# Attention passes: the projection's blocks one block later, and the forget gate's chain spread over four blocks

## What is computed

```python
def mixer_fox_nsa(h, w_in, b_f, cmp_pe, cmp_w1, cmp_w2, w_out):
    proj = h @ w_in
    fq, fk, fv, ff, nq, kc, vc, ks, vs, kw, vw, ng = [proj[..., offs[i]:offs[i + 1]] for i in range(len(IN_SIZES))]
    log_f = jax.nn.log_sigmoid((ff + b_f).astype(jnp.float32))
    o_fox = fox_attention(fq.reshape(hd), fk.reshape(hd), fv.reshape(hd), log_f)
    gates = jax.nn.sigmoid(ng.astype(jnp.float32)).astype(h.dtype).reshape(B, S, NSA_KV_GROUPS, NSA_GROUP_SIZE, 3)
    o_nsa = nsa_attention(nq, kc, vc, ks, vs, kw, vw, gates, cmp_pe, cmp_w1, cmp_w2)
    return jnp.concatenate([o_fox, o_nsa], axis=-1) @ w_out
```

## Time and profile before

| | |
|---|---|
| median of 3 runs | 1832.21 us (1831.14 to 1836.81) |
| the profiled execution | 1836.81 us, span 1835.1 us |
| busy PE / DVE / ACT / POOL | 1723.6 / 911.9 / 657.8 / 183.2 us |
| mean granted PE clock | 0.963 |
| att5 to the last pass, in the trace | about 660 to 975 us |

### The profile page before, as it was taken

One profiled execution on the slowest core, in us unless ns is written; L12 is line 12 of the kernel. 1 busy time (PEld: TensorE's weight loads), 2 busy tenths in 40 slices (PEclk: granted clock), 3 DMA queues, 4 the chain that ended last, 5 costly groups with the idle time before them and its releaser, 6 DMA issues.

```text
span 1835.1 us, 22072 instructions
## 1 busy us (share of the span) xinstructions
PE 1723.6 (94%) x8153; PEld 1348.1 (73%) x8153; DVE 911.9 (50%) x1368; ACT 657.8 (36%) x937; POOL 183.2 (10%) x178
## 2 busy tenths in 40 slices
PE   1999899999999989999999899999999899999996
PEld 1657678888888766666656688888887688888885
DVE  6865674533333361555666644444335744444223
ACT  1324334444322241354555344443224433333221
POOL 4001119910000050000000000001100000000000
PEclk9999889999999989999999799999998799999998
DMA  7554155522322241111102122223222032323221
GB/s 280 206 192 161 47 183 172 179 96 94 118 79 94 73 106 46 58 36 35 36 24 69 58 92 99 95 92 117 95 74 80 12 103 91 103 91 115 93 78 46
DMA packets 49111, 179.73 MB, mean 98 GB/s; under 512 B 5984, under 2 KB 6656, under 8 KB 48928
## 3 DMA queue, kind: packets, MB, share of 16 engines
q1 hardware_dynamic: 44896, 166.75, 27.0%
q0 software_dynamic: 3008, 10.59, 2.1%
q10 hardware_dynamic: 1152, 1.66, 0.3%
HBM read 173.56 MB, written 2.10 MB: 96 GB/s over the span
## 4 chain that ended last, share of the span: by engine, by line
PE 66%; issue 22%; DVE 8%; ACT 2%; DMA 1%; ACTq 1%; POOL 1%; DVEq 0%; POOLq 0%; SPq 0%
PE bank L332 15%; PE bank L333 15%; PE bank L334 15%; PE bank L1195 3%; PE bank L1197 2%; PE bank L1196 2%; PE bank L1299 2%; PE bank L1275 2%; PE bank L1255 1%; DVE ada_acc L1652 1%; PE bank L1180 1%; PE bank L1353 1%; DMA raw<-in_ada_w 1%; DVE w_lo L271 1%; ACT w_hi L267 1%
## 5 line engine op out<-in xcount | busy, mean ns | idle before, releaser
L271 DVE TENSOR_TENSOR w_lo<-raw,w_hi 128x1024 fp32r<-128x1024 f32 (+1 forms) x236 | 319.0, 1352 | 673.2 <-ACT w_hi L267 673.0
L332 PE MATMUL bank<-h_hi,w_hi 128*128 128x512 f32 x1232 | 488.7, 397 | 4.8 <-DVE h_lo L519 1.5
L333 PE MATMUL bank<-h_lo,w_hi 128*128 128x512 f32 x1232 | 482.6, 392 | 0.0
L334 PE MATMUL bank<-h_hi,w_lo 128*128 128x512 f32 x1232 | 481.9, 391 | 0.0
L267 ACT ACTIVATE w_hi<-raw 128x1024 fp32r<-128x1024 f32 (+1 forms) x236 | 265.3, 1124 | 574.0 <-PE bank L334 505.6
L332 PEld LDWEIGHTS bank<-h_hi,w_hi 128*128 128x128 f32 x1232 | 232.8, 189 | 63.1 <-issue 6.4
L334 PEld LDWEIGHTS bank<-h_hi,w_lo 128*128 128x128 f32 x1232 | 233.0, 189 | 49.4
L333 PEld LDWEIGHTS bank<-h_lo,w_hi 128*128 128x128 f32 x1232 | 233.2, 189 | 47.9 <-issue 1.0
L332 PE MATMUL bank<-hid_hi,w_hi 128*128 128x512 f32 x528 | 209.7, 397 | 0.0
L333 PE MATMUL bank<-hid_lo,w_hi 128*128 128x512 f32 x528 | 209.4, 397 | 0.0
L334 PE MATMUL bank<-hid_hi,w_lo 128*128 128x512 f32 x528 | 209.3, 396 | 0.0
(11 more groups left out here) (325 smaller groups left out, 1953.0 us busy)
## 6 DMA issues: line engine op xcount, KB each, us to landing
raw<-in_f2i SPq DMA_DIRECT2D x88, 512.0 KB, 3.2
raw<-in_ffi SPq DMA_DIRECT2D x44, 512.0 KB, 3.3
raw<-in_f2o SPq DMA_DIRECT2D x32, 704.0 KB, 4.0
ada_w<-in_ada_w SPq DMA_DIRECT2D x32, 512.0 KB, 4.0
raw<-in_att_w SPq DMA_DIRECT2D x24, 512.0 KB, 3.2
raw<-in_ffo SPq DMA_DIRECT2D x16, 704.0 KB, 4.0
raw<-in_ada_w SPq DMA_DIRECT2D x16, 512.0 KB, 5.0
raw<-in_w_in SPq DMA_DIRECT2D x16, 512.0 KB, 5.3
```

What stands on the lines that cost most here:

```text
L271: nc.vector.tensor_tensor(WL[par][:, 0:kc * P], RAW[s][:, 0:kc * P], WH[par][:, 0:kc * P].bitcast(F32), ALU.subtract).then_inc(wlo, 1)
L332: pe_.matmul(bank[:, :], w_h, hi[:, k0 + k, :], start=start and k == 0, stop=False)
L333: pe_.matmul(bank[:, :], w_h, lo[:, k0 + k, :], start=False, stop=False)
L334: last = pe_.matmul(bank[:, :], w_l, hi[:, k0 + k, :], start=False, stop=stop and k == kc - 1)
```

## The change

Three things. The passes get a table of steps per slot (STEPS): pass 0 has 24 steps, passes 1 to 3 have 32 of which the first 8 belong to the NQ block of their own pair, and pass 4 has that block's 8. `att_block` stands where the table says a block has ended (`ready_at`), one slot later, except for NQ and for a block that ends in slot 15. In `att_block`, DVE copies the bank out before it makes w_lo. The transposes of V come in slot 1, and DVE's saved output behind the first scores. In att5 PE transposes gates and V one block later, and the forget gate's chain is cut into pieces at blocks (0, 0) to (1, 1).

```diff
+        STEPS = [[2] * 12 + [0] * 4] + [[3, 3, 2, 2, 2, 2, 1, 2, 2, 2, 1, 2, 2, 2, 2, 2]] * 3 + [[3, 3, 2] + [0] * 13]
+        EARLY_AT = 3
+        chunk_of, ready_at, _n = {}, {}, 0
+        for _p in range(5):
+            for _sl in range(SLOTS):
+                chunk_of[_p, _sl] = range(_n, _n + STEPS[_p][_sl])
+                _n += STEPS[_p][_sl]
+                for _s in chunk_of[_p, _sl]:
+                    if _s % C == C - 1:
+                        late = 0 if _s // C % 4 == 3 or _p == 0 or _sl == SLOTS - 1 else 1
+                        ready_at.setdefault((_p, _sl + late), []).append(_s // C)
...
             lin("att5", 0, 2)
+            lin("att5", 0, 3)
             pe_.wait_ge(a5["ng"], 1)
             for i in range(TC):
                 m = pe_.transpose(PS[5][:, i * P:i * P + 3 * NH], NG[:, i * P:(i + 1) * P], IDN[0:3 * NH, 0:3 * NH])
             m.then_inc(a5["ngt"], 1)
-            lin("att5", 0, 3)
...
-            v_turn(VST, PS[4], ev[1], O0["att5"] // 2 + 3, a5["vt"], VF)
...
                 hidden(CMPB - 4, CMPB).then_inc(a5["hc"], 1)
+                if kv == 0:
+                    v_turn(VST, PS[4], ev[1], O0["att5"] // 2 + 3, a5["vt"], VF)
...
-                    if p < 4:
-                        lin_step("att6", 4 * p + sl // 4, 2 * (sl % 4))
-                    elif sl == 1:
+                    steps = chunk_of[p, sl]
+                    ahead = (len(steps) + 1) // 2
+                    for s_ in steps[:ahead]:
+                        lin_step("att6", s_ // C, s_ % C)
+                    if p == 4 and sl == EARLY_AT:
                         pe_.wait_ge(a6["ol"], 6)
-                    if p == 4 and 1 <= sl <= 12:
-                        j, e = divmod(sl - 1, 6)
+                    if p == 4 and EARLY_AT <= sl < EARLY_AT + 12:
+                        j, e = divmod(sl - EARLY_AT, 6)
...
-                        if sl == 0:
+                        if sl == 1:
                             fv_turn(it)
                         if sl < NP_:
                             qk(it, sl)
-                    if p < 4:
-                        lin_step("att6", 4 * p + sl // 4, 2 * (sl % 4) + 1)
+                    for s_ in steps[ahead:]:
+                        lin_step("att6", s_ // C, s_ % C)
...
-                    if sl % 4 == 0:
-                        if sl and p < 4:
-                            att_block(4 * p + sl // 4 - 1)
-                        elif sl == 0 and p:
-                            att_block(4 * p - 1)
+                    for j in ready_at.get((p, sl), ()):
+                        att_block(j)
...
-                split_lo(N0["att6"] + j + 2, t % 2, (t + 2) % 4, C)
                 dve.wait_ge(mm, N0["att6"] + j + 1)
...
+                split_lo(N0["att6"] + j + 2, t % 2, (t + 2) % 4, C)
...
+                        if sl < NP_:
+                            score(it, sl)
                         if sl == 0 and it:
                             out_lo(it - 1, 1)
-                        if sl < NP_:
-                            score(it, sl)
```

More of the change, by code:

```diff
@@ L1483, in beside5 @@
             def beside5(g, t):
-                if (g, t) == (0, 0):
+                if (g, t) == (0, 1):
+                    act.wait_ge(ev[1], O0["att5"] // 2 + 1)
+                    act.activation(NG, NG, ACT.Sigmoid).then_inc(a5["ng"], 1)
+                elif (g, t) == (0, 2):
                     act.wait_ge(a5["abs"], 1)
@@ L1488, in beside5 @@
                     act.activation(LA, LE, ACT.Ln, bias=1.0).then_inc(a5["lnx"], 1)
-                elif (g, t) == (0, 1):
-                    act.wait_ge(ev[1], O0["att5"] // 2 + 1)
-                    act.activation(NG, NG, ACT.Sigmoid).then_inc(a5["ng"], 1)
-                elif (g, t) == (1, 1):
+                elif (g, t) == (1, 2):
                     act.wait_ge(a5["vt"], 1)
@@ L1561, in _ @@
                     else:
-                        if sl == 0:
-                            if it:
-                                out_hi(it - 1, 1)
+                        if sl == 0 and it:
+                            out_hi(it - 1, 1)
+                        if sl == 1:
                             act.wait_ge(a6["fvt"], it + 1)
@@ L1872, in evac5 @@
                     dve.tensor_scalar(LX, LX, BF[:, 0:1], None, ALU.add).then_inc(a5["xf"], 1)
+                elif (g, t) == (0, 1):
+                    dve.tensor_tensor(NG, bank[0:3 * NH, :], RQ0[0:3 * NH, :], ALU.mult).then_inc(ev[1], 1)
                     dve.wait_ge(a5["xf"], 1)
@@ L1875, in evac5 @@
                     dve.memset(LF[:, :], 1.0).then_inc(a5["lf"], 1)
-                    dve.wait_ge(a5["lnx"], 1)
-                    dve.scalar_tensor_tensor(LE, LX, 0.0, LA, ALU.min, ALU.subtract).then_inc(a5["lf"], 1)
-                    dve.wait_ge(a5["lf"], 2)
-                    dve.tensor_tensor_scan(LF[:, :], ONES_ROW, LE, 0.0, ALU.mult, ALU.add).then_inc(a5["cs"], 1)
-                elif (g, t) == (0, 1):
-                    dve.tensor_tensor(NG, bank[0:3 * NH, :], RQ0[0:3 * NH, :], ALU.mult).then_inc(ev[1], 1)
                 elif g == 1:
@@ L1897, in evac5 @@
                                       pe_v[:, :, 16:32].to_broadcast([P, NCMP, 16]), ALU.add).then_inc(a5["ke"], 1)
-                    if kv == 0:
-                        dve.wait_ge(a5["ngt"], 1)
-                        dve.tensor_copy(GT[:, :, :], PS[5][:, :].rearrange("p (i t) -> p i t", i=TC)[:, :, 0:3 * NH]).then_inc(a5["ctc"], 1)
-                        dve.wait_ge(const_ready, 3)
-                        dve.memset(CR[:, :].bitcast(F32), 0.0).then_inc(a5["cr"], 1)
-                        dve.tensor_copy(SELB[:, :, :], SI[:, :].rearrange("p (h t) -> p h t", t=1).to_broadcast([P, NH, P])).then_inc(a5["cr"], 1)
-                        dve.wait_ge(a5["cr"], 1)
-                        dve.wait_ge(a5["cs"], 1)
-                        for r in (0, 64):
-                            dve.tensor_copy(CR[r:r + NH, :], LF[:, :]).then_inc(a5["ctc"], 1)
-                        dve.wait_ge(a5["ctc"], 2)
-                        for r in (32, 96):
-                            dve.tensor_tensor(CR[r:r + NH, :], LF[:, :], CR[0:NH, :].bitcast(F32), ALU.subtract).then_inc(a5["cr"], 1)
+                if (g, t) == (0, 3):
+                    dve.wait_ge(a5["lnx"], 1)
+                    dve.scalar_tensor_tensor(LE, LX, 0.0, LA, ALU.min, ALU.subtract).then_inc(a5["lf"], 1)
+                    dve.wait_ge(a5["lf"], 2)
+                    dve.tensor_tensor_scan(LF[:, :], ONES_ROW, LE, 0.0, ALU.mult, ALU.add).then_inc(a5["cs"], 1)
+                elif (g, t) == (1, 0):
+                    dve.wait_ge(const_ready, 3)
+                    dve.memset(CR[:, :].bitcast(F32), 0.0).then_inc(a5["cr"], 1)
+                    dve.tensor_copy(SELB[:, :, :], SI[:, :].rearrange("p (h t) -> p h t", t=1).to_broadcast([P, NH, P])).then_inc(a5["cr"], 1)
+                elif (g, t) == (1, 1):
+                    dve.wait_ge(a5["ngt"], 1)
+                    dve.tensor_copy(GT[:, :, :], PS[5][:, :].rearrange("p (i t) -> p i t", i=TC)[:, :, 0:3 * NH]).then_inc(a5["ctc"], 1)
+                    dve.wait_ge(a5["cr"], 1)
+                    dve.wait_ge(a5["cs"], 1)
+                    for r in (0, 64):
+                        dve.tensor_copy(CR[r:r + NH, :], LF[:, :]).then_inc(a5["ctc"], 1)
+                    dve.wait_ge(a5["ctc"], 2)
+                    for r in (32, 96):
+                        dve.tensor_tensor(CR[r:r + NH, :], LF[:, :], CR[0:NH, :].bitcast(F32), ALU.subtract).then_inc(a5["cr"], 1)
```

## The result

The changed kernel takes 1811.0 us in the median of four executions (1807.6 to 1811.6), against 1831.7 us for the kernel before, measured beside it. The ratio is 0.9874, 95% interval [0.9855, 0.9894]: 23.1 us less of the 1832.2 us shown before, between 19.4 and 26.6 (the two medians alone differ by 20.6). The forecast was 1816 us, 16 us less. The profiled execution took 1811.5 us, its span 1809.8 us at a mean granted clock of 0.970 (0.963 before).

The account below looks back on a forecast made before the run. TensorE (PE) and its issue, 88% of the chain, bound the kernel; 5.6 + 3.4 + 4.7 + 3.4 + 1.5 + 1.1 = 19.7 us gave 1817.1, or 1815.9 from the median with half the low clock: forecast 1816 us. Range 1811.8 to 1820.2, near 1809 lowest, 1824 with (a).

Parts of the forecast that it names:

- att5, 5.6 us of waits and 3.4 us of clock: K/V projection stage: PE's waits for gates (2.50 us) and V block (3.07 us) go, with two low-clock stretches, 3.4 us.
- the cover named for the forget gate's chain: att5: chain spread over blocks 2 to 5, row tile first read over 50 us later, so costed at nothing.
- Passes, 8.9 us gone: Passes: five PE waits at the fox score products (L1250) for DVE's scores, 8.9 us together, would go.
- 0.85 us in slot 4, in three passes; in the last pass ... 1.65 us: Passes: new PE wait in slot 4 behind the NQ copy and w_lo, together 4.2 us, leaving net 4.7 us.
- Neither bound: Slot 4's new wait: from nothing (ACT makes w_hi before the exponentials) to 2.8 us a pass (w_hi, w_lo, copy in a row).
- Four waits at L1270, three gone: Transposes of the compressed scores: three of four PE waits of about 0.5 us go, 1.5 us saved.
- two at L1275 gone: Slots 13 and 14 of the last pass: waits of 0.6 and 0.5 us go through one att_out step each, 1.1 us.
- Low clock, 6.8 us in the sum: Four low-clock stretches behind removed waits go: 3.4 us for two in att5, 3.4 us for two at pass starts.
- If such a run had only half of the low-clock stretches that I count: Step from the profiled execution to the median: 1832.2 - 12.9 - 3.4 = 1815.9 us.
- (b): Rival, passes: DVE's slot 2 costs PE 2.8 us in each of four passes, low clock too; 1826.7 us; chance 0.09.
- (c): Rival, slots 2 and 15: PE meets DVE's 2.8 us seven times, each with 1.7 us low clock; 1844.4 us; chance 0.03.
- (a): Rival: waits go, but as many low-clock stretches fall behind remaining waits; 1823.9 us, or 1819.3 from the median; chance 0.14.

Follow-up runs that it names:

- the two versions above: Changed kernel with the split that goes with NQ at the end of slot 5: 0.9864, 1809.2 us; or NQ's copy and split one slot later: 0.9856, 1806.9 us.
- early steps in slots 1 to 12: Changed kernel with the twelve early steps of att_out back in slots 1 to 12 of the last pass: 1813.6 us in one execution.
- forget gate's chain at once: Changed kernel with the forget gate's exp, ln and scan back at block (0, 0), transposes left a block later: att5 takes 55.8 us in place of 53.3.
- passes alone: Kernel before with only the passes' part of the change, att5 as before: ratio 0.9943, 10.5 us less.

## Why the prediction was right and wrong

- **att5, 5.6 us of waits and 3.4 us of clock**: right. The stage is 9.0 us shorter, alone or with the rest, and the cover named for the forget gate's chain held. That the sum needs both edits, the transposes and the spread chain, was implied ("no exp and ln ahead of it now") and is shown.
- **Passes, 8.9 us gone, "0.85 us in slot 4, in three passes; in the last pass ... 1.65 us"**: right, 0.81 three times and 1.55. The chain of rows from slot 2's product, 8.1 us, took 8.14 (852.28 to 860.42), and PE's own work 7.3 against 7.25. Neither bound came, nothing or 2.8 us; one slot later would have made it nearly nothing, 0.3 us once.
- **Four waits at L1270, three gone; two at L1275 gone**: right, 2.1 - 0.7 = 1.4 us against 1.5, and 1.1.
- **Low clock, 6.8 us in the sum**: each stretch stands in it with 1.7 us, which the windows of the earlier trace rows give as (1 - 0.66) x 5 or (1 - 0.87) x 13; by the time of a pass one cost 1.5 us. The four named stretches did go, but behind two of the new waits came one each of 3.4 us, about 1.7 us lost apiece by the same reckoning, in two of three profiles, one in the third. So the changed stages gave 3.4 to 5.1 us of it. The forecast had not priced its own new waits with the clock. With those waits gone (the two versions above) there was none.
- **The step that failed is the low-clock term, on the way from the sum to the median**: "If such a run had only half of the low-clock stretches that I count", 12.9 + 3.4 = 16.3 us, with nothing for low clock outside the changed stages. The waits, 12.9 us, were right (13.0 in the profile, 12.4 by the means). The clock gave 9.3 us in the mean where the forecast had 3.4, and the gain was 20 to 23 us. The halving had as its only ground that the profiled execution was the slowest of three. The kernel before varies from 1827 to 1838 us with its mean granted clock (0.972 to 0.962), and its profiled execution says little of how many of the four stretches a median run has. What was missing lies elsewhere: 3.4 is within what the changed stages gave, and the other 4 to 6 us came from stages with the same code, for which the forecast had no term. The runs do not show why. That the whole sum, 19.7, lies near the measured 20 to 23 is therefore luck in part.
- The low end of 1809 us was too near as well. Its own terms give 1811.8 - 3.4 = 1808.4; 0.9874 of the 1832.2 us shown is 1809.1, the interval's low end 1805.6.
- **"A given wait does not always bring one"**, read from one pair of windows, was seen again: with the same four waits the changed kernel's clock fell at 861.6 and 919.6 in its first profile, at 858.9 and 916.9 in its second, and only at 752.0 in its third.
- **The rivals**: (b), the wait only moves, is out: 1 us and not 2.8 in each pass. So is (c). (a), low clock behind waits that remain, happened in part, with 1.7 to 3.4 us, not behind the 1.01 us at block 2 but behind the new ones.

## What to carry to other kernels

Here a wait that a reordering leaves was computed to 0.1 us from the rows of one stretch whose order stays the same, engine by engine; do this first, and then try the split one slot further, where it cost nothing. Removing 13 us of short waits of PE gave 20 to 23 us: count the lower clock behind each wait (here 1.5 us where it came), behind the ones you create as well, and do not cut the sum only because the profiled execution is the slowest shown. Keep the range open downward for low clock in stages that you do not touch. Compare those stages before crediting an edit, and do not read a cause from one profile of a stage whose low time changes from one execution to the next.

## What the runs showed of the hardware

- In the changed kernel's first profile the granted clock fell to 0.50 for 3.4 us at 861.6 and at 919.6, behind PE waits of 0.81 us (ended at 860.42) and 1.55 us (917.87). In other executions with the same waits it did not, or fell elsewhere. Of the seven profiles with the four new waits, three had 6.8 us of it in the passes (the changed kernel's first and second, V transposes in slot 0), three 3.4 us (the changed kernel's third, early steps in slots 1 to 12, forget gate's chain at once) and one none (passes alone). The six with neither these waits nor the five of the kernel before had none: 1.00 over 660:960. One such fall cost 1.5 us: pass 3 took 57.45 us with it (first profile) and 55.95 without (third). Inside such a stretch of the kernel before, matmuls of 512 columns start 0.43 us apart, at 1.00 0.23 us.
- In the stretch after the attention, low-clock stretches stand at nearly the same places in every kernel, about 42, 424, 457 and 842 us after its start, and each is longer or shorter from one profile to another, by 3.4 us or a little more. Together they are 60.5 to 71.3 us long, and the same instructions take 856.4 to 859.7 us. The sum goes with where the stretch meets the changes of the clock: 60.5 to 60.7 where the first begins 41.3 to 41.6 us in, 71.0 to 71.3 where it begins 40.4 to 41.2 us in. Two profiles that begin it at 958.9 and 959.3 us have 71.1 and 64.8.
- A group of chunk steps (three 512-column matmuls each) set apart between fp32 products cost about 0.05 us more than one joined to its neighbour, estimated from 27 groups fewer.
